# End of the eight FFNs in a two-block decoder kernel: a third buffer for the inner values, other order of the last down products, down weights of the last piece split in column halves

## The chip, the cores and the metric

One Trainium2 chip, one core. The time is the device time of one execution in microseconds (us). Three runs of the kernel before are known, with the median 2170.97 us. The profile is of one execution of its own, taken by the hardware profiler. Engines are named as in the profile: PE (TensorE, matrix products), PEld (its weight loads), DVE (VectorE), ACT (ScalarE), POOL (GpSimd), SP (SyncE, which here only issues DMAs).

## The reference

The input is 256 tokens of width 1024. Two model blocks, each of depth 2, run one behind the other. Every layer has two feed-forward networks (FFN) of inner width 2816 around a mixer, so there are eight FFNs. The part that the change touches is the FFN, and, in the second block's even mixer, the places of three small constant masks.

```python
def rmsnorm(x, g):
    xf = x.astype(jnp.float32)
    y = xf * lax.rsqrt(jnp.mean(xf * xf, axis=-1, keepdims=True) + EPS)
    return (y * g.astype(jnp.float32)).astype(x.dtype)

def swiglu_ffn(x, w_gu, w_down):
    gate, up = jnp.split(x @ w_gu, 2, axis=-1)
    return (jax.nn.silu(gate) * up) @ w_down

for i in range(DEPTH):
    x = x + 0.5 * swiglu_ffn(rmsnorm(x, ffn1_norm[i]), ffn1_w_gu[i], ffn1_w_down[i])
    xn = rmsnorm(x, mix_norm[i])
    x = x + mixer(xn, ...)
    x = x + 0.5 * swiglu_ffn(rmsnorm(x, ffn2_norm[i]), ffn2_w_gu[i], ffn2_w_down[i])
...
# second block, even mixer, gated delta rule in chunks of 64:
t_inv = lax.linalg.triangular_solve(a_low + eye, jnp.broadcast_to(eye, a_low.shape),
                                    left_side=True, lower=True, unit_diagonal=True)
```

## The kernel before

The stages run in the order f1.0, ab, f2.0, f1.1, nsa, f2.1, g1.0, ev, g2.0, pl0, g1.1, od, g2.1, pl1. Those named f or g are the FFNs: f2.0 and f2.1 have another FFN right behind them, the other six a mixer or a "ple" stage.

Every float32 product is made of three products of rounded parts: a value v is kept as its high part H (rounded by a copy to the type fp32r) and its low part L = v - H, and `mm3` adds H times H, H times L and L times H. So each weight costs ACT a copy (`hi`, into the tile WH) and DVE or POOL a subtraction (`lo`, into WL). Weights come in pieces through a ring of three slots, filled by SP in one fixed order. SP waits with a slot's next load until the low parts of its old contents are made.

**An FFN.** It has 22 pieces j. A piece holds 128 inner columns: 1024 weight columns for the gate product (part 0), 1024 for the up product (part 1), and 1024 for the down product (part 2). Per piece PE makes gate j, up j, and then the down products of piece j - 2, which wait for nothing by then. In between ACT and DVE form the inner value h = silu(gate) * up in `H`, its high part in `HH` and its low part in `HL` (the tiles HHt and HLt), each with two buffers that take turns by j % 2. A down product is `down(P, j, n, i)`: column half n (512 of the 1024 output columns) for the token half i (128 of 256 tokens), three matmuls with 512 columns each. The four accumulate in four banks of PSUM over all pieces (`acc00`, `acc10`, `acc01`, `acc11`).

**The end of an FFN** in the kernel before. In the last piece (21) PE makes the gate product, then the four down products of piece 19, then the up product. Behind it stand three of the four down products of piece 20 (nine matmuls), then `down_last(0)`, the six matmuls of piece 21 for the first column half, which wait for h's high part of each token half and only then for its low part; then the fourth down product of piece 20; then `follow[t].pe(P, 0)`, eight transposes of the first half of the new X ("flips" here) for the next stage; then `down_last(1)`. DVE adds the finished banks to X: `fin00` and `fin10` release the adds that the flips wait for. From the flips' results ACT and DVE make the next stage's input parts XH and XL (tile XBt), on which the next stage's first product waits.

ACT makes the high part of the last down weights (`hi(A, f"{t}.{j}", (2,))`) between the silu and the copy of the up product, as in every piece; DVE makes their low part right behind its gate work.

What sets the order of the work is the program order of each engine: no scheduler stands between. Semaphore waits are written by name.

**The masks.** In the even mixer POOL adds the left and the right half of three constant tables (`lev`, `bdT`, the identity) into `LEV`, `BD` and `ID` in the tile work before the solve. The constants come in two DMAs; the second, `ct1`, with 2173 columns, is issued by SP behind the loads of piece 3 and ahead of those of piece 4.

Of the kernel before, what the change touches and what calls it, by code (L numbers as in the profile page):

```python
# [6 lines left out]
F32 = mybir.dt.float32  # L7
# [17 lines left out]
def plan():  # L25
# [30 lines left out]
       ("cmneg", 30), ("mask4", 512), ("cos", 32), ("sin", 32), ("blk", 128), ("one1", 1)]  # L56

# [190 lines left out]
def build(nc, wts, vecs, rows4, rowb, cons, rgw, xin, out):  # L248
    ctx = ExitStack()
    with ctx:  # L250
# [3 lines left out]
        CO, NC = offsets(CON)  # L254
# [4 lines left out]
        HHt, HLt = sb("HHt", [128, 512], R32), sb("HLt", [128, 512], R32)  # L259
# [456 lines left out]
        def ffn(t, g, prev):  # L716
# [3 lines left out]
            HH, HL = v3(HHt[:, :], 2), v3(HLt[:, :], 2)  # L720
# [3 lines left out]
            def down(P, j, n, i):  # L724
                piece = f"{t}.{j}"
                wh, wl = wide(piece)
                P.wait_ge(f"{t}.hl{j}", f"{piece}:lo2", *ps.free(f"{t}.acc{i}{n}"), f"{t}.rbe")
                ws = slice(2048 + n * 512, 2560 + n * 512)
                P.mm3(ps[f"{t}.acc{i}{n}"], HH[:, j % 2, hs(i)], HL[:, j % 2, hs(i)], wh[:, ws], wl[:, ws], j == 0, False,
                      inc=f"{piece}:d" if n and i else None)  # L730

            def down_last(P, n):

                j, piece = NFF - 1, last
                wh, wl = wide(piece)
                ws = slice(2048 + n * 512, 2560 + n * 512)
                P.wait_ge(f"{piece}:lo2")
                for i in range(2):
                    P.wait_ge(f"{t}.hh{j}{i}")
                    P.mm(ps[f"{t}.acc{i}{n}"], HH[:, j % 2, hs(i)], wh[:, ws], False, False)  # L740
                    P.mm(ps[f"{t}.acc{i}{n}"], HH[:, j % 2, hs(i)], wl[:, ws], False, False)
                for i in range(2):
                    P.wait_ge(f"{t}.hl{j}{i}")
                    P.mm(ps[f"{t}.acc{i}{n}"], HL[:, j % 2, hs(i)], wh[:, ws], False, True,
                         inc=f"{piece}:d" if n and i else f"{t}.fin{i}{n}")
# [17 lines left out]
            def pe(P):  # L763
                if first:
                    norm.pe(P, 0)
                for j in range(NFF):
                    for u in range(2):
                        ps.take(f"{t}.{'gu'[u]}{j}")
                    for kts in (range(2), range(2, 4), range(4, 6), range(6, 8)) if j == 0 else (range(8),):
                        for u in range(2):  # L770
                            P.wait_ge(f"{t}.{j}:lo{u}", *ps.free(f"{t}.{'gu'[u]}{j}"))
                            if j == 1 and u == 1:
                                product(P, j, u, range(4))
                                row_pe(P, t, f"{t}.acc11")
                                product(P, j, u, range(4, 8))
                            else:
                                product(P, j, u, kts)
                            if j == NFF - 1 and u == 0:
                                for n in range(2):
                                    for i in range(2):  # L780
                                        down(P, j - 2, n, i)
                        if j == 0 and kts[0] == 0:
                            norm.pe(P, 1)
# [8 lines left out]
                for n, i in ((0, 0), (0, 1), (1, 0)):  # L792
                    down(P, NFF - 2, n, i)
                down_last(P, 0)
                down(P, NFF - 2, 1, 1)
                for i in range(2):
                    ps.give(f"{t}.acc{i}0", f"{t}.x{i}0")
                if t in follow:
                    follow[t].pe(P, 0)
# [4 lines left out]
            def act(A):  # L804
# [6 lines left out]
                for j in range(NFF):  # L811
# [7 lines left out]
                    hi(A, f"{t}.{j}", (2,))  # L819
# [5 lines left out]
                    if j < NFF - 1:  # L825
                        A.wait_ge(f"{t}.h{j}")
                        if j >= 2:
                            A.wait_ge(f"{t}.{j - 2}:d")
                        A.act(HH[:, b, :], H[:, b, :], ACT.Copy, inc=f"{t}.hh{j}")
                    else:  # L830
                        for i in range(2):
                            A.wait_ge(f"{t}.h{j}{i}", f"{t}.{j - 2}:d")
                            A.act(HH[:, b, hs(i)], H[:, b, hs(i)], ACT.Copy, inc=f"{t}.hh{j}{i}")
                        hi(A, nx2, (1,))
# [6 lines left out]
            def dve(V):  # L841
# [7 lines left out]
                for j in range(NFF):  # L849
# [13 lines left out]
                    lo(V, f"{t}.{j}", (2,))  # L863
# [25 lines left out]
                for i in range(2):  # L889
                    V.wait_ge(f"{t}.hh{j}{i}")  # L890
                    V.tt(HL[:, b, hs(i)], H[:, b, hs(i)], HH[:, b, hs(i)].bitcast(F32), SUB, inc=f"{t}.hl{j}{i}")
# [157 lines left out]
        def ab_mixer(prev):  # L1049
# [29 lines left out]
            YH, YL = v3(HHt[:, :], 2), v3(HLt[:, :], 2)  # L1079
# [889 lines left out]
        def even_mixer(prev):  # L1969
# [22 lines left out]
            LEV, BD, ID = v3(at(11776, 384), 6), at(12160, 64), at(12224, 64)  # L1992
# [554 lines left out]
            def dve(V):  # L2547
# [70 lines left out]
                for i in range(2):  # L2618
                    V.wait_ge(f"ev.xe{i}", "ev.blocks")
# [73 lines left out]
            def pool(G_):  # L2693
                G_.wait_ge(f"{t}.dg")
                G_.tt(LEV, v3(con("lev"), 6)[:, :, 0:64], v3(con("lev"), 6)[:, :, 64:128], ADD)
                G_.tt(BD, bdT[:, 0:64], bdT[:, 64:128], ADD, back=2)
                G_.tt(ID, IDN[:, 0:64], IDN[:, 64:128], ADD, inc="ev.blocks", back=3)
# [396 lines left out]
        def sync(S):  # L3094
# [8 lines left out]
            for name, n, two in PL:  # L3103
# [40 lines left out]
                if k == 3:  # L3144
                    S.dma(ct[:, 256:], cons[:, 256:], "cons1", inc="ct1")
# [213 lines left out]
```

## Time and profile before

| what | value |
|---|---|
| median of three runs | 2170.97 us (2170.86 to 2172.56) |
| span of the profiled execution, first to last instruction | 2171.1 us |
| PE busy | 2117.3 us, 98% of the span |
| DVE, ACT busy | 1548.0 us (71%), 1291.5 us (59%) |
| POOL busy | 73.2 us (3%) |
| moved by DMA | 363.00 MB, mean 167 GB/s |

The profiled execution has no time of its own beside its span; the span stands 0.1 us above the median of the runs. A busy share of 98% leaves PE about 54 us without an instruction in the whole program (2171.1 less 2117.3).

The rows below are in three forms. In a timeline a row begins with the start in us and the length of the row in us; behind them come engine, line and operation, out<-in by the tiles' names, and in brackets how long the engine sat idle before and what ended that. Matmuls overlap in such rows (one of 0.39 us may be followed by the next 0.23 us later), so it is starts that are compared, not lengths. In a table by form a row ends with busy us, mean ns of one, and idle time before. In a table of waits: us in total, times, longest.

### The profile page before, as it was taken

How to read it: one execution, taken by the hardware profiler on the slowest of the kernel's cores; microseconds unless marked ns; L12 is line 12 of the kernel's file. 1: busy time of each engine (PE TensorE's matmuls, PEld its weight loads, DVE VectorE, ACT ScalarE, POOL GpSimd, SP SyncE). 2: the span in 40 equal slices, each digit the busy share in tenths (PEclk: the TensorE clock that was granted, in tenths of full speed). 3: DMA queues.
4: the chain of work that ended last, by engine and by line, in shares of the span. 5: the costliest groups of instructions: out<-in, count | busy, mean ns of one | idle time of the engine just before them, and what ended most of it. 6: DMA issues, size and time to landing. Idle time of an engine off the chain costs nothing.

```text
span 2171.1 us, 33763 instructions
## 1 busy us (share of the span) xinstructions
PE 2117.3 (98%) x12655; PEld 1810.4 (83%) x12655; DVE 1548.0 (71%) x2771; ACT 1291.5 (59%) x2165; POOL 73.2 (3%) x49
## 2 busy tenths in 40 slices
PE   8999999999999989999999999999999999999998
PEld 7888988888888966888788897888887888988887
DVE  6777887677776576776777766577666776867676
ACT  6665766555555266655565666456555655666554
POOL 0001000000002300000000000000000000000001
PEclk9999999999999999999999998999999999999999
DMA  7453445554554532455455341145544554435552
GB/s 269 176 204 141 150 172 182 197 186 166 202 183 163 198 123 78 175 196 192 149 201 200 115 166 60 60 152 209 183 160 175 204 197 153 156 146 187 182 200 81
DMA packets 65532, 363.00 MB, mean 167 GB/s; under 512 B 7576, under 2 KB 8344, under 8 KB 33880
## 3 DMA queue, kind: packets, MB, share of 16 engines
q1 hardware_dynamic: 64944, 360.31, 46.1%
q8 instruction: 99, 1.62, 0.3%
q14 instruction: 65, 0.53, 0.1%
q0 software_dynamic: 128, 0.26, 0.0%
q10 hardware_dynamic: 296, 0.27, 0.0%
HBM read 359.77 MB, written 1.05 MB: 166 GB/s over the span
## 4 chain that ended last, share of the span: by engine, by line
PE 84%; DVE 10%; ACT 4%; issue 1%; DMA 0%; DVEq 0%; POOL 0%; ACTq 0%; SPq 0%; POOLq 0%
PE ps L202 83%; DVE WL L120 4%; PE ps L207 2%; DVE work L120 1%; ACT work L192 1%; ACT XBt L192 1%; DVE XBt L131 1%; ACT WH L192 1%; DVE small L131 1%; DVE work L131 1%; DVE small L120 1%; DVE work L157 0%; DVE work L125 0%; DVE small L127 0%; DVE XBt L120 0%
## 5 line engine op out<-in xcount | busy, mean ns | idle before, releaser
L202 PE MATMUL ps<-XBt,WH 128*128 128x512 f32 (+1 forms) x4208 | 1213.4, 355 | 13.2 <-DVE WL L120 6.6
L120 DVE TENSOR_TENSOR WL<-ring,WH 128x1024 fp32r<-128x1024 f32 (+1 forms) x642 | 789.3, 1229 | 364.3 <-ACT WH L192 320.3
L192 ACT ACTIVATE WH<-ring 128x1024 fp32r<-128x1024 f32 (+1 forms) x662 | 701.3, 1059 | 336.8 <-PE ps L202 269.5
L202 PE MATMUL ps<-XBt,WL 128*128 128x256 f32 x3384 | 896.0, 280 | 0.0
L202 PEld LDWEIGHTS ps<-XBt,WH 128*128 128x128 f32 x4208 | 729.4, 190 | 122.7 <-DVE XBt L131 9.8
L202 PEld LDWEIGHTS ps<-XBt,WL 128*128 128x128 f32 x3384 | 641.8, 190 | 26.2
L202 PE MATMUL ps<-WH,HHt 128*128 128x512 f32 x712 | 279.3, 392 | 1.3 <-DVE WL L120 0.7
L202 PE MATMUL ps<-WL,HHt 128*128 128x512 f32 x712 | 277.2, 389 | 0.0
L202 PE MATMUL ps<-WH,HLt 128*128 128x512 f32 x712 | 274.6, 389 | 0.0
L192 ACT ACTIVATE work<-ps 128x256 f32<-128x256 f32 (+5 forms) x457 | 184.3, 408 | 76.6 <-PE ps L202 39.6
L192 ACT ACTIVATE work<-work 128x256 f32<-128x256 f32 (+6 forms) x221 | 98.3, 445 | 183.3 <-DVE work L120 179.9
L120 DVE TENSOR_TENSOR work<-ps,work 128x256 f32<-128x256 f32 (+3 forms) x376 | 166.2, 442 | 42.9 <-PE ps L202 3.3
L202 PE MATMUL ps<-WH,XBt 128*128 128x512 f32 (+3 forms) x528 | 169.6, 391 | 12.9 <-DVE WL L120 11.1
L192 ACT ACTIVATE HHt<-work 128x256 fp32r<-128x256 f32 (+1 forms) x185 | 76.1, 411 | 147.0 <-DVE work L120 146.9
L202 PEld LDWEIGHTS ps<-WH,HLt 128*128 128x128 f32 x712 | 133.7, 188 | 28.9
L202 PEld LDWEIGHTS ps<-WL,HHt 128*128 128x128 f32 x712 | 133.8, 188 | 28.3
L202 PEld LDWEIGHTS ps<-WH,HHt 128*128 128x128 f32 x712 | 133.7, 188 | 24.2 <-DVE work L120 1.7
L120 DVE TENSOR_TENSOR work<-work 128x256 f32<-128x256 f32 (+2 forms) x338 | 142.8, 423 | 12.3 <-ACT work L192 0.7
L202 PEld LDWEIGHTS ps<-WH,XBt 128*128 128x128 f32 x528 | 99.9, 193 | 37.6 <-DVE WL L120 12.0
L120 POOL TENSOR_TENSOR WL<-ring,WH 128x1024 fp32r<-128x1024 f32 x22 | 53.8, 2448 | 1952.7 <-DVE HLt L120 1410.5
L202 PE MATMUL ps<-work 64*64 64x64 f32 (+16 forms) x1256 | 115.7, 278 | 3.9 <-ACT work L192 1.9
L202 PEld LDWEIGHTS ps<-work 64*64 64x64 f32 (+6 forms) x1256 | 87.5, 156 | 26.9 <-issue 10.9
(132 smaller groups left out, 1152.2 us busy)
## 6 DMA issues: line engine op xcount, KB each, us to landing
ring<-wts SPq DMA_DIRECT2D x244, 1024.0 KB, 5.9
ring<-wts SPq DMA_DIRECT2D x187, 512.0 KB, 3.8
ring<-wts SPq DMA_DIRECT2D x1, 1152.0 KB, 5.1
ct<-cons SPq DMA_DIRECT2D x1, 1086.5 KB, 5.8
Xt<-x SPq DMA_DIRECT2D x4, 256.0 KB, 5.3
out<-Xt SPq DMA_DIRECT2D x4, 256.0 KB, 2.0
work<-wts SPq DMA_DIRECT2D x1, 512.0 KB, 4.7
ring<-wts SPq DMA_DIRECT2D x1, 288.0 KB, 5.1
```

What stands on the lines that cost most here:

```text
L120: self.done(self.e and self.e.tensor_tensor(out, a, b, op), inc)
L131: self.done(self.e and self.e.scalar_tensor_tensor(out, a, s, b, op0, op1), inc)
L192: self.done(self.e and self.e.activation(out, a, f, **kw), inc)
L202: inst = self.e and self.e.matmul(out, l, r, start=start, stop=stop)
L207: inst = self.e and self.e.transpose(out, a, ident)
```

## The change

HHt and HLt grow from two buffers to three; the third is used by the last piece alone. The four down products of piece 19 are moved behind the last up product too, where those of piece 20 stood already, and two of piece 20's now stand between `down_last(0)` and the flips. The order behind the up product is four of piece 19, two of piece 20 (column half 0), `down_last(0)`, two of piece 20 (column half 1), flips, `down_last(1)`. `down_last` now waits for h's low part and uses `mm3`. The last down weights are split into high and low part in two halves of 512 columns, on both engines behind the work on h. The masks' half tables are loaded by DMA into the places where they are used, in seven more DMAs from the same source; POOL's three additions and the wait for them are gone.

```diff
+HALF = {"lev": 384}
+CHIP = [(n, HALF.get(n, c)) for n, c in CON] + [("bd2", 64), ("id2", 64)]
...
-        HHt, HLt = sb("HHt", [128, 512], R32), sb("HLt", [128, 512], R32)
+        HHt, HLt = sb("HHt", [128, 768], R32), sb("HLt", [128, 768], R32)
...
             def down_last(P, n):
...
-                P.wait_ge(f"{piece}:lo2")
-                for i in range(2):
-                    P.wait_ge(f"{t}.hh{j}{i}")
-                    P.mm(ps[f"{t}.acc{i}{n}"], HH[:, j % 2, hs(i)], wh[:, ws], False, False)
-                    P.mm(ps[f"{t}.acc{i}{n}"], HH[:, j % 2, hs(i)], wl[:, ws], False, False)
+                P.wait_ge(f"{piece}:lo2{'' if n else 'a'}")
                 for i in range(2):
                     P.wait_ge(f"{t}.hl{j}{i}")
-                    P.mm(ps[f"{t}.acc{i}{n}"], HL[:, j % 2, hs(i)], wh[:, ws], False, True,
-                         inc=f"{piece}:d" if n and i else f"{t}.fin{i}{n}")
+                    P.mm3(ps[f"{t}.acc{i}{n}"], HH[:, 2, hs(i)], HL[:, 2, hs(i)], wh[:, ws], wl[:, ws], False, True,
+                          inc=f"{piece}:d" if n and i else f"{t}.fin{i}{n}")
+
+            def split_last_act(A, n):
+
+                wh, _, w = cut(last, 2)
+                s = slice(n * 512, n * 512 + 512)
+                A.wait_ge(loaded(last, 2), f"{t}.{NFF - 3}:d{'' if n else '0'}")
+                A.act(wh[:, s], w[:, s], ACT.Copy, inc=f"{last}:hi2{'' if n else 'a'}")
+
+            def split_last_dve(V, n):
+                wh, wl, w = cut(last, 2)
+                s = slice(n * 512, n * 512 + 512)
+                V.wait_ge(f"{last}:hi2{'' if n else 'a'}")
+                V.tt(wl[:, s], w[:, s], wh[:, s].bitcast(F32), SUB, inc=f"{last}:lo2{'' if n else 'a'}")
...
-                            if j == NFF - 1 and u == 0:
-                                for n in range(2):
-                                    for i in range(2):
-                                        down(P, j - 2, n, i)
...
-                for n, i in ((0, 0), (0, 1), (1, 0)):
-                    down(P, NFF - 2, n, i)
+                for n in range(2):
+                    for i in range(2):
+                        down(P, NFF - 3, n, i)
+                for i in range(2):
+                    down(P, NFF - 2, 0, i)
                 down_last(P, 0)
-                down(P, NFF - 2, 1, 1)
                 for i in range(2):
                     ps.give(f"{t}.acc{i}0", f"{t}.x{i}0")
+                for i in range(2):
+                    down(P, NFF - 2, 1, i)
                 if t in follow:
                     follow[t].pe(P, 0)
                 down_last(P, 1)
...
-                            A.wait_ge(f"{t}.h{j}{i}", f"{t}.{j - 2}:d")
-                            A.act(HH[:, b, hs(i)], H[:, b, hs(i)], ACT.Copy, inc=f"{t}.hh{j}{i}")
+                            A.wait_ge(f"{t}.h{j}{i}")
+                            A.act(HH[:, 2, hs(i)], H[:, b, hs(i)], ACT.Copy, inc=f"{t}.hh{j}{i}")
+                        for n in range(2):
+                            split_last_act(A, n)
                         hi(A, nx2, (1,))
...
+                for n in range(2):
+                    split_last_dve(V, n)
...
-                G_.wait_ge(f"{t}.dg")
-                G_.tt(LEV, v3(con("lev"), 6)[:, :, 0:64], v3(con("lev"), 6)[:, :, 64:128], ADD)
-                G_.tt(BD, bdT[:, 0:64], bdT[:, 64:128], ADD, back=2)
-                G_.tt(ID, IDN[:, 0:64], IDN[:, 64:128], ADD, inc="ev.blocks", back=3)
...
-                    S.dma(ct[:, 256:], cons[:, 256:], "cons1", inc="ct1")
+                    a, b = offsets(CON)[0], offsets(CON)[1]
+                    lev, tail = a["lev"][0], a["cm01"][0]
+                    S.dma(ct[:, 256:lev], cons[:, 256:lev], "cons1")
+                    for e in range(2):
+                        r = slice(64 * e, 64 * e + 64)
+                        S.dma(v3(con("lev")[r, :], 6), v3(cons[r, lev:tail], 6)[:, :, 64 * e:64 * e + 64], "cons1")
+                        S.dma(con("bd2")[r, :], cons[r, a["bdT"][0] + 64 * e:a["bdT"][0] + 64 * e + 64], "cons1")
+                        S.dma(con("id2")[r, :], cons[r, 64 * e:64 * e + 64], "cons1")
+                    S.dma(ct[:, tail - 384:CO["bd2"][0]], cons[:, tail:b], "cons1", inc="ct1")
```

PE at the end of the first FFN (f1.0), before. Here ps6 and ps7 are the banks acc00 and acc10 (column half 0), ps0 and ps1 are acc01 and acc11. The rows begin with the third down product of piece 20, behind the last up product:

```order
L202 MATMUL ps0<-WH,HHt 128x512
L202 MATMUL ps0<-WL,HHt 128x512
L202 MATMUL ps0<-WH,HLt 128x512
L202 MATMUL ps6<-WH,HHt 128x512 [waits scalar_done,vector_done]
L202 MATMUL ps6<-WL,HHt 128x512
L202 MATMUL ps7<-WH,HHt 128x512 [waits scalar_done]
L202 MATMUL ps7<-WL,HHt 128x512
L202 MATMUL ps6<-WH,HLt 128x512 [waits vector_done]
L202 MATMUL ps7<-WH,HLt 128x512 [waits vector_done]
L202 MATMUL ps1<-WH,HHt 128x512
L202 MATMUL ps1<-WL,HHt 128x512
L202 MATMUL ps1<-WH,HLt 128x512
```

PE at the same place, after, from the second down product of piece 20 to the third. Ahead of these rows stand the up product and fifteen more matmuls of down products:

```order
L204 MATMUL ps7<-WH,HHt 128x512
L204 MATMUL ps7<-WL,HHt 128x512
L204 MATMUL ps7<-WH,HLt 128x512
L204 MATMUL ps6<-WH,HHt 128x512 [waits vector_done]
L204 MATMUL ps6<-WL,HHt 128x512
L204 MATMUL ps6<-WH,HLt 128x512
L204 MATMUL ps7<-WH,HHt 128x512
L204 MATMUL ps7<-WL,HHt 128x512
L204 MATMUL ps7<-WH,HLt 128x512
L204 MATMUL ps0<-WH,HHt 128x512
L204 MATMUL ps0<-WL,HHt 128x512
L204 MATMUL ps0<-WH,HLt 128x512
```

The last piece's first half has one wait now in place of four, on DVE's low parts; it stands behind 18 matmuls of down products instead of nine, counted from the end of the up product, and six matmuls instead of three follow it before the flips.

ACT at the same place, before, from the silu of piece 21 (work<-work) on:

```order
L192 ACTIVATE work<-work 128x256 [waits scalar_done,vector_done]
L192 ACTIVATE WH<-ring 128x1024 [waits scalar_done,matmul_done,rear0]
L192 ACTIVATE work<-ps5 128x256 [waits scalar_done,matmul_done]
L192 ACTIVATE HHt<-work 128x128 [waits scalar_done,vector_done] x2
L192 ACTIVATE WH<-ring 128x1024 [waits scalar_done]
```

and after:

```order
L194 ACTIVATE work<-work 128x256 [waits scalar_done,vector_done]
L194 ACTIVATE work<-ps5 128x256 [waits scalar_done,matmul_done]
L194 ACTIVATE HHt<-work 128x128 [waits scalar_done,vector_done] x2
L194 ACTIVATE WH<-ring 128x512 [waits scalar_done,matmul_done,rear0]
L194 ACTIVATE WH<-ring 128x512 [waits scalar_done,matmul_done]
L194 ACTIVATE WH<-ring 128x1024 [waits scalar_done]
```

The high part of the last down weights has moved from ahead of the copy of the up product (work<-ps5) to behind the high part of h, in two halves. DVE's low part has moved in the same way.

SP in the first FFN, after; before, the six rows on ct are one, `L195 DMA ct<-cons 128x2173`:

```order
L197 DMA ring<-wts 128x2048 [waits vector_done]
L197 DMA ring<-wts 128x1024 [waits vector_done]
L197 DMA ct<-cons 128x640
L197 DMA ct<-cons 64x6x64
L197 DMA ct<-cons 64x64 x2
L197 DMA ct<-cons 64x6x64
L197 DMA ct<-cons 64x64 x2
L197 DMA ct<-cons 128x765
L197 DMA ring<-wts 128x2048
```

The load of piece 4's gate and up weights (the last row) stands behind eight DMAs of constants instead of one.

## Rows read from the trace of the kernel before

**Rows 1.** The page: its head, and the chain that ended last, by engine

```profile
span 2171.1 us, 33763 instructions
...
PE 84%; DVE 10%; ACT 4%; issue 1%; DMA 0%; DVEq 0%; POOL 0%; ACTq 0%; SPq 0%; POOLq 0%
```

**Rows 2.** Waits of PE over the whole span, longest in total

```profile
PE ps L202 <- DVE WL L120: 18.4, 14, 3.8
```

**Rows 3.** Timeline, end of f2.0 (an FFN follows): PE and ACT

```profile
497.65 0.42 ACT L192 ACTIVATE work<-work 128x256 f32<-128x256 f32 x1 [0.80 <-DVE work L120]
...
499.57 0.40 PE L202 MATMUL ps<-WH,HHt 128*128 128x512 f32 x1
...
502.26 0.47 PE L202 MATMUL ps<-WH,HHt 128*128 128x512 f32 x1 [0.47 <-ACT HHt L192]
...
504.63 1.31 PE L207 MATMUL ps<-ct,Xt 128*128 128x128 f32 x8
505.70 0.48 PE L202 MATMUL ps<-WH,HHt 128*128 128x512 f32 x1
...
507.56 0.50 PE L202 MATMUL ps<-XBt,WH 128*128 128x256 f32 x2 [0.23 <-DVE XBt L131]
```

**Rows 4.** Timeline, end of f1.1 (a mixer follows): ACT, DVE and PE

```profile
685.05 0.42 ACT L192 ACTIVATE work<-work 128x256 f32<-128x256 f32 x1
...
687.69 0.40 PE L202 MATMUL ps<-WH,HHt 128*128 128x512 f32 x1
687.89 0.39 ACT L192 ACTIVATE work<-ps 128x256 f32<-128x256 f32 x1 [1.25 <-PE ps L202]
...
689.68 0.69 DVE L120 TENSOR_TENSOR HLt<-work,HHt 128x128 fp32r<-128x128 f32 x2
689.75 0.39 PE L202 MATMUL ps<-WH,HHt 128*128 128x512 f32 x1
...
691.89 1.31 PE L207 MATMUL ps<-ct,Xt 128*128 128x128 f32 x8
692.96 0.48 PE L202 MATMUL ps<-WH,HHt 128*128 128x512 f32 x1
...
696.36 1.04 PE L207 MATMUL ps<-ct,Xt 128*128 128x128 f32 x8
...
697.32 0.50 PE L202 MATMUL ps<-XBt,WH 128*128 128x256 f32 x2
```

**Rows 5.** Timeline, ends of f2.1 (two rows) and g1.0 (three rows)

```profile
1044.99 0.40 PE L202 MATMUL ps<-WH,HHt 128*128 128x512 f32 x1
...
1050.77 0.48 PE L202 MATMUL ps<-WH,HHt 128*128 128x512 f32 x1
...
1234.31 0.42 ACT L192 ACTIVATE work<-work 128x256 f32<-128x256 f32 x1 [0.64 <-DVE work L120]
...
1236.40 0.40 PE L202 MATMUL ps<-WH,HHt 128*128 128x512 f32 x1
...
1242.02 0.48 PE L202 MATMUL ps<-WH,HHt 128*128 128x512 f32 x1
```

**Rows 6.** Groups by form, whole span: work of 512 columns on ACT and DVE

```profile
L192 ACT ACTIVATE work<-Xt 128x512 f32<-128x512 f32 x60 | 38.0, 633 | 6.1 <-DVE Xt L120 0.5 <-DVE XBt L131 0.4
...
L120 DVE TENSOR_TENSOR work<-ps,work 128x512 f32<-128x512 f32 x24 | 16.6, 692 | 4.7 <-PE ps L202 2.3 <-DVE small L139 0.5
```

**Rows 7.** Timeline, first FFN: SP's DMA issues, then ACT, DVE, PE

```profile
30.05 0.44 SPq L195 DMA_DIRECT2D ct<-cons  x1
30.53 0.43 SPq L195 DMA_DIRECT2D ring<-wts  x1
...
38.39 1.06 ACT L192 ACTIVATE WH<-ring 128x1024 fp32r<-128x1024 f32 x1 [2.29 <-DMA ring<-wts]
...
43.48 1.23 DVE L120 TENSOR_TENSOR WL<-ring,WH 128x1024 fp32r<-128x1024 f32 x1
...
46.77 0.63 PE L202 MATMUL ps<-XBt,WH 128*128 128x512 f32 x2
```

More of the change, by code:

```diff
@@ L253, in build @@
         RO, NR = offsets(ROW)
-        CO, NC = offsets(CON)
+        CO, NC = offsets(CHIP)
         ring = sb("ring", [128, NSLOT * SLOT])
@@ L719, in ffn @@
             SG, H, GU, LW = v3(buf(512), 2), v3(buf(512), 2), v3(buf(1024), 2), v3(buf(1024), 2)
-            HH, HL = v3(HHt[:, :], 2), v3(HLt[:, :], 2)
+            HH, HL = v3(HHt[:, :], 3), v3(HLt[:, :], 3)
             first = t == "f1.0"
@@ L729, in down @@
                 P.mm3(ps[f"{t}.acc{i}{n}"], HH[:, j % 2, hs(i)], HL[:, j % 2, hs(i)], wh[:, ws], wl[:, ws], j == 0, False,
-                      inc=f"{piece}:d" if n and i else None)
+                      inc=f"{piece}:d" if n and i else f"{piece}:d0" if i and j == NFF - 3 else None)
             def down_last(P, n):
@@ L818, in act @@
                     A.act(SG[:, b, :], GU[:, b, 0:256], ACT.Silu, inc=f"{t}.sg{j}")
-                    hi(A, f"{t}.{j}", (2,))
+                    if j < NFF - 1:
+                        hi(A, f"{t}.{j}", (2,))
                     if j >= NARROW:
@@ L862, in dve @@
                         lo(V, nx2, (0,) if j else (1,))
-                    lo(V, f"{t}.{j}", (2,))
+                    if j < NFF - 1:
+                        lo(V, f"{t}.{j}", (2,))
                     V.wait_ge(f"{t}.sg{j}")
@@ L890, in dve @@
                     V.wait_ge(f"{t}.hh{j}{i}")
[L891 removed]
+                    V.tt(HL[:, 2, hs(i)], H[:, b, hs(i)], HH[:, 2, hs(i)].bitcast(F32), SUB, inc=f"{t}.hl{j}{i}")
+                for n in range(2):
+                    split_last_dve(V, n)
                 for n in range(2):
@@ L1078, in ab_mixer @@
             wif, wil = HHt[:, 0:64], HLt[:, 0:64]
-            YH, YL = v3(HHt[:, :], 2), v3(HLt[:, :], 2)
+            YH, YL = v3(HHt[:, 0:512], 2), v3(HLt[:, 0:512], 2)
             def if_pe(P):
@@ L1991, in even_mixer @@
                                          for a in (11264, 12288, 13312, 14336, 15360, 16384)]
-            LEV, BD, ID = v3(at(11776, 384), 6), at(12160, 64), at(12224, 64)
+            LEV, BD, ID = v3(con("lev"), 6), con("bd2"), con("id2")
             WT, S_ = two_(2048), at(3072, 512)
@@ L2618, in dve @@
                 for i in range(2):
-                    V.wait_ge(f"ev.xe{i}", "ev.blocks")
+                    V.wait_ge(f"ev.xe{i}")
                     for h in range(4):
```

## Prediction

> **What bounds the kernel now.** I read the page's head and its chain first, then PE's waits, then the timelines of all eight FFN ends, then the start, where SP's order changes. The span is 2171.1 us and 84% of the chain that ended last is PE itself [rows 1]. So time goes only where PE's matmul count goes (this change leaves it as it is) or where PE stands still. PE's longest sum of waits is for low parts of weights made by DVE, 18.4 us in 14 places [rows 2]. At the FFN ends, where this change works, PE waits far less, and that is the point on which everything hangs.
>
> I call U the start of the first down product behind the last up product, and D the start of `down_last(1)`, behind the flips. From U to D PE has 18 matmuls of 512 columns and eight transposes. At the end of f1.1, U is 687.69, `down_last(0)` starts at 689.75 after nine matmuls (2.06 us, 0.229 us each, so without a wait), and D is 692.96 [rows 4]: U to D is 5.27 us. Four other ends (f1.0, g2.0, g1.1, g2.1) have the same shape with 5.27 or 5.28 us. At the end of f2.0 `down_last(0)` starts at 502.26, 2.69 us behind U at 499.57, after the same nine matmuls: a stall of 0.63 us for h's high part, and more inside `down_last(0)`, since D is 505.70, U plus 6.13 us [rows 3]. For f2.1 U to D is 5.78 us, for g1.0 it is 5.62 us [rows 5]. So five of the eight ends have next to nothing to gain, and the other three hold 0.96, 0.61 and 0.45 us above a floor that I work out now.
>
> **The floor.** 18 matmuls at 0.229 us are 4.12 us. Nine plus nine before bring the f1.1 flips to 687.69 + 4.12 = 691.81; they start at 691.89, so 0.08 us goes on the change of work. The flips then take 1.07 us to D there, because their second token half waits for X; the next stage's flips, which wait for nothing, take 0.96 us (696.36 to 697.32), and their own rows say the same, 1.04 against 1.31 us [rows 4]. After the change X's two adds are ready before the flips, since six matmuls (1.37 us) stand between `down_last(0)` and them. The floor is 4.12 + 0.08 + 0.96 = 5.16 us.
>
> **When can the new `down_last(0)` start?** PE reaches it after the four down products of piece 19 and two of piece 20. U's meaning shifts with the change: the up product now comes 12 matmuls earlier, and the instant at which piece 19's products end and those of piece 20 begin is where U was. So PE reaches `down_last(0)` at U + 6 x 0.229 = U + 1.37 us. It needs h's low part and the low part of the first 512 columns of the down weights.
>
> The up product ends 2.7 us earlier, yet ACT cannot take it at once: it sits in the silu of piece 21, which waits for DVE and which the change doesn't touch. From the silu's end on: ACT copies the up product, then comes the work on h. Before, from the start of that copy to the end of h's low parts, it is 687.89 to 689.68 + 0.69 = 690.37, so 2.48 us [rows 4]. ACT's new half copy begins about 0.45 us before that end (at the end of h's second high part) and takes 0.63 us; DVE's half subtraction follows 0.04 us later and takes 0.69 us [rows 6]. That is the copy's start plus 2.48 - 0.45 + 0.63 + 0.04 + 0.69, about 3.4 us.
> - f1.1: silu from 685.05, 0.42 long, copy at 685.51, low part at 688.93. PE arrives at 687.69 + 1.37 = 689.06. No stall, with some 0.08 us to spare after 0.05 us of signalling. The same at the four ends of its shape.
> - f2.0: silu from 497.65, copy at 498.11, low part at 501.53, PE arrives at 500.94. A stall of 0.59, plus 0.13 us for the signal and the slower first matmul behind a wait: 0.72 us. f2.1 has the shape of f2.0, and I give it the same 0.72 us.
> - g1.0: silu from 1234.31, copy at 1234.77, low part at 1238.19, PE arrives at 1237.77: 0.42 + 0.13 = 0.55 us.
>
> So the change cuts the chain by less than it seems: it brings the up product forward by 2.7 us, but it moves the down weights' split behind h, and makes PE wait for all low parts where before it could start on the high ones.
>
> **The sum at the FFN ends**, each against U to D before: five ends 5.16 against 5.27, 0.11 us gained each, 0.55 in all. f2.0: 5.16 + 0.72 = 5.88 against 6.13, 0.25 gained. f2.1: 5.88 against 5.78, 0.10 lost. g1.0: 5.71 against 5.62, 0.09 lost. Net gain 0.61 us. Behind D the next product waits for the flips' way over ACT and DVE, 1.86 us from D at f2.0 (505.70 to 507.56), and not for `down_last(1)` [rows 3]. That way is unchanged and starts with the flips, so a shift of D passes on whole and no more is to be had. The bounds of this term: with no stall anywhere it gains 0.55 + 0.97 + 0.62 + 0.46 = 2.6 us; if DVE could begin only when ACT has made both halves (0.67 us later), it loses about 5 x 0.59 + 3 x 0.67 - 0.6 = 4.4 us. I take 0.61, since both half durations have rows of their own size.
>
> What else moves at the ends: the last piece's low down part frees its ring slot about 1.8 us later, so where an FFN follows, SP issues two loads later. They serve pieces 2 and 3 of the next FFN, wanted more than 10 us behind; cost nothing. POOL's splits for the next mixer start earlier, which nobody waits for. The third buffers take away a wait of ACT for piece 19's products, which in the new order would have come late; by themselves they gain nothing.
>
> **The start.** SP issues the constants at 30.05 in 0.44 us and piece 4's load at 30.53 [rows 7]. Seven more DMAs at 0.43 us put that load about 3.0 us later. Before, it queued behind more than a megabyte of constants and landed when ACT's wait ended, at 38.39 [rows 7]; so issued 3 us later it finds the queue nearly empty, and I expect it to land between 0 and 3 us later. What lies over it: DVE's last low part made from that load runs 43.48 to 44.71, and the up product that needs it starts at 47.00, the second matmul of the row at 46.77 [rows 7]. That is 2.3 us of cover. No row of before shows such a strided load by SP. At three us of delay the cost is 0.7 us (3.0 - 2.3); if each of the seven takes twice the issue time of the row, the load is 6.0 us late and costs 3.7 us. I take 0, by the queue that is empty by then. The bytes shrink a little, so below zero there is nothing but tenths, and those are covered as well.
> The Trainium skill speaks against these small DMAs ("DMA: Bandwidth & Descriptors", section Bandwidth): it advises large transfers and calls those under 64 KB "descriptor-dominated"; its table has 64 KB at 0.95 us. Four of the new ones are 16 KB and two 98 KB. By an estimate from that page, some 0.9 us for each of six, one behind the other, the load would land up to 5.4 us later and the sum would be 2173.5 instead. No row here shows it either way.
>
> **The masks.** POOL's three additions and DVE's wait for them go. POOL is in 0% of the chain [rows 1], they are done long before they are read, and the removed wait had been met. Cost and gain 0.
>
> **Sum:** 2171.1 - 0.61 = 2170.5 for the profiled span. That span stands 0.1 above the median of 2170.97, so in terms of the median 2170.4 us.
>
> **Rivals.**
> 1. *The low parts come late (slower).* Place: the first matmul of `down_last(0)`, all eight ends. If the chain of h and the half splits is x us longer than I reckon, three ends lose x and five lose x - 0.08. The gain of 0.61 is gone at x = 0.13. For it: the slack at five ends is a twelfth of a microsecond, and ACT and DVE must take turns four times within it. Against: every link has a measured duration. With x = 0.35 the time is 2170.4 + 8 x 0.35 - 0.4 = 2172.8; at its bound, 0.67, it is 2175.4.
> 2. *The constants' DMAs hold up piece 4 (slower).* It decides from 2.3 us of delay on, and outweighs the gain from 2.9 us. For it: ACT already waited 2.29 us for this load before the change [rows 7], so it is the tightest load of the program. With the 6.0 us from above PE loses 3.7 us: 2170.4 + 3.7 = 2174.1. Against: the bytes are fewer, and the load is alone in the queue once it is issued.
> 3. *All stalls go (faster).* If silu 21 ended earlier too, or DVE took the half split sooner, every end would sit on the floor: 2171.0 - 2.6 = 2168.4. For it: the up product is 2.7 us earlier. Against: silu 21 hangs on the gate work, which stands where it stood.
> 4. *Nothing reaches the end.* If the ACT and DVE way behind the flips also waits for something else, the tenths vanish: 2171.0. It can't be told from the forecast.
>
> **Chances.** Forecast with rival 4: 0.74 (own range 2169.4 to 2171.8). Rival 1: 0.11. Rival 2: 0.07. Rival 3: 0.08. A measurement can tell from no change about 0.2%, 4.3 us, so faster means under 2166.6 and slower over 2175.3. No worked case reaches the first, only the far end of rival 1 or rivals 1 and 2 together reach the second. For what I have overlooked I leave 0.04 faster, 0.05 slower, 0.91 within. The range, 2168.2 to 2173.4, takes in rival 3, the middle of rival 1 and rival 2 up to 5.3 us of delay.
>
> **What would show it.** In the profile after: U to D of 5.2 us at the five ends, with no wait ahead of `down_last(0)`; 5.9 at f2.0 and f2.1 and 5.7 at g1.0, with a wait for DVE's WL of about 0.6 us there; D to the next product still 1.86 us; piece 4's high part in the first FFN at 38 to 41 us, and PE without a gap near 47. Wrong would be: waits for DVE WL at all eight ends (rival 1), a gap at 44 to 50 us (rival 2), or ends of 5.2 us everywhere (rival 3).

## The result, and the profile after

| | kernel before | changed kernel |
|---|---|---|
| median of the runs | 2170.91 us (2169.51 to 2172.56, 4 runs) | 2188.63 us (2183.20 to 2189.84, 4 runs) |
| span of the profiled execution | 2171.1 us | 2186.2 us (its time as a run: 2187.99) |

The changed kernel takes 1.0072 times as long, with the interval 1.0061 to 1.0084: 13 to 18 us slower. The medians are 17.7 us apart, the spans of the two profiled executions 15.1 us. The forecast was 2170.4 us, with a range of 2168.2 to 2173.4.

The head of the page after, with its line of the chain (engine, busy us, share, instructions):

```profile
span 2186.2 us, 33797 instructions
...
PE 2116.9 (97%) x12655; PEld 1810.6 (83%) x12655; DVE 1565.9 (72%) x2779; ACT 1291.9 (59%) x2173; POOL 72.4 (3%) x46
...
PE 79%; DVE 12%; ACT 6%; issue 2%; DMA 0%; SPq 0%; DVEq 0%; ACTq 0%; POOL 0%; POOLq 0%
```

Against [rows 1] PE has the same work (2116.9 against 2117.3 us), so nearly all of the 15.1 us is time in which it stands still. DVE has become 17.9 us busier (1565.9 against 1548.0), though the change gives it no more to subtract. The table of waits and the table by form say where. First PE's waits for DVE's low parts after the change (us, times, longest), against 18.4 us in 14 before [rows 2]:

```profile
PE ps L204 <- DVE WL L122: 30.9, 23, 3.8
```

Then, of the table by form, the half splits that the change made (busy us, mean ns; idle before):

```profile
L122 DVE TENSOR_TENSOR WL<-ring,WH 128x512 fp32r<-128x512 f32 x16 | 29.2, 1825 | 3.5 <-ACT WH L194 2.6
```

An operation of this size had a row with 692 ns before [rows 6]; here the sixteen have a mean of 1825 ns. They cost 29.2 where 16 x 0.692 = 11.1 us were due: 18.1 us too much, which accounts for the 17.9 us that DVE gained. The timeline of the end of f1.1 shows a case (start, length, what):

```profile
691.89 0.69 DVE L122 TENSOR_TENSOR HLt<-work,HHt 128x128 fp32r<-128x128 f32 x2
...
692.17 0.39 PE L204 MATMUL ps<-WH,HHt 128*128 128x512 f32 x1
...
692.72 5.16 POOL L122 TENSOR_TENSOR WL<-ring,WH 128x1024 fp32r<-128x1024 f32 x2 [473.00 <-DVE HLt L122]
...
692.91 5.52 DVE L122 TENSOR_TENSOR WL<-ring,WH 128x512 fp32r<-128x512 f32 x2 [0.33 <-ACT WH L194]
...
695.69 0.50 PE L204 MATMUL ps<-WH,HHt 128*128 128x512 f32 x1 [2.00 <-DVE WL L122]
...
698.55 1.41 DVE L133 SCALAR_TENSOR_TENSOR Xt<-ps,small,Xt 128x512 f32<-128x512 f32 x2
...
699.35 1.32 PE L209 MATMUL ps<-ct,Xt 128*128 128x128 f32 x8 [0.65 <-DVE Xt L133]
...
700.42 0.48 PE L204 MATMUL ps<-WH,HHt 128*128 128x512 f32 x1
```

POOL waits for h's low part (the semaphore `{t}.hl{NFF - 1}1`) before it makes two splits for the next mixer. DVE has to wait a little longer, for ACT's high part. So POOL starts at 692.72 and DVE at 692.91, 0.19 us behind; DVE's first half then takes 2.73 us and ends at 695.63, 0.55 us behind POOL's first split, and PE stands still for 2.00 us ahead of `down_last(0)`. POOL's second split is then in progress, so DVE's second half takes as long again; behind it come the adds into X, and the flips wait 0.65 us more. From U (692.17) to D (700.42) it is 8.25 us, where 5.27 stood before [rows 4].

Where no such POOL split is ready, the forecast holds. The same place at f2.0, whose next stage is another FFN:

```profile
504.39 0.39 PE L204 MATMUL ps<-WH,HHt 128*128 128x512 f32 x1
...
505.83 1.49 DVE L122 TENSOR_TENSOR WL<-ring,WH 128x512 fp32r<-128x512 f32 x2 [0.33 <-ACT WH L194]
...
506.58 0.50 PE L204 MATMUL ps<-WH,HHt 128*128 128x512 f32 x1 [0.66 <-DVE WL L122]
...
509.46 1.04 PE L209 MATMUL ps<-ct,Xt 128*128 128x128 f32 x8
510.25 0.48 PE L204 MATMUL ps<-WH,HHt 128*128 128x512 f32 x1
```

Both halves in 1.49 us, a wait of 0.66 us, and U to D is 5.86 us; the forecast was 5.88, with [rows 3] at 6.13. The five ends at which POOL starts a split right behind h's low part (f1.0, f1.1, g2.0, g1.1, g2.1) have the long wait of f1.1, with one difference: at g1.1 POOL makes a single split, so that only DVE's first half is held up (both halves together take 3.46 us there, against 5.52 at f1.1). The other three are like f2.0. At g1.0 POOL has a split too, but it waits for ACT and starts at 1245.64, behind DVE's halves (1243.63 to 1245.12). U to D of each in us, starts of matmuls compared as in the prediction (6.12 and 5.77 are from unrounded starts; the rows give 6.13 and 5.78):

| | f1.0 | f2.0 | f1.1 | f2.1 | g1.0 | g2.0 | g1.1 | g2.1 |
|---|---|---|---|---|---|---|---|---|
| before | 5.27 | 6.12 | 5.27 | 5.77 | 5.62 | 5.27 | 5.27 | 5.27 |
| forecast | 5.16 | 5.88 | 5.16 | 5.88 | 5.71 | 5.16 | 5.16 | 5.16 |
| changed | 8.88 | 5.86 | 8.25 | 5.86 | 5.66 | 8.20 | 8.68 | 8.20 |

From U to the next stage's first product, the eight ends together grow from 59.07 to 75.14 us, by 16.1. Two of the five bad ends, f1.0 and g1.1, lose half a microsecond more than the others, g1.1 although only one half was held up. There the clock fell. The table of windows gives the granted clock behind the engines' busy times:

```profile
200.20:203.40 3.20, 3.20 (x10) 2.42 (x9) 2.75 (x3) 0.00 (x0) 0.80 (x1) 0.50 0.62 256
...
1855.70:1858.90 3.20, 3.20 (x9) 2.46 (x8) 1.50 (x2) 0.00 (x0) 0.00 (x0) 0.50 0.72 289
```

0.50 is 1.2 GHz, half of 2.4. In these 3.2 us, which begin about 1 us after PE's wait ended (1.4 us at f1.0, 0.8 at g1.1), matmuls of 512 columns start 0.43 us apart instead of 0.23. At g1.1 it is 5.23 us from `down_last(0)` to D, where the same stretch takes 3.65 us at the full clock in `pool_behind` below, so about 1.6 us of that end is the clock. At f1.0 it is about 0.5 us (5.25 us from `down_last(0)` to D against 4.73 at f1.1), since the flips wait for X there anyway.

The start is the second place. SP's constants and the loads behind them, and ACT's high part of the first piece 4 load, against [rows 7]:

```profile
30.02 5.10 SPq L197 DMA_DIRECT2D ct<-cons  x8
...
35.16 24.93 SPq L197 DMA_DIRECT2D ring<-wts  x9
...
41.82 1.06 ACT L194 ACTIVATE WH<-ring 128x1024 fp32r<-128x1024 f32 x1 [5.75 <-DMA ring<-wts]
...
48.19 0.50 PE L204 MATMUL ps<-XBt,WH 128*128 128x512 f32 x1 [0.91 <-DVE WL L122]
```

Eight DMAs took SP 5.10 us, 0.64 each and not 0.43; the high part began at 41.82 instead of 38.39, and PE stood still for 0.91 us. U of f1.0 is 1.3 us later than before (195.19 against 193.88). So the ledger of the span is +16.1 at the ends, +1.3 at the start, and 15.1 - 16.1 - 1.3 = -2.3 us in the mixers between. The change doesn't touch that part, and the profiles differ there by as much anyway: `masks_alone` (below) has the same ends as before and a start 0.4 us later, and yet a span of 2168.1 us, 3 less. Of the 2.3 us, 1.7 lie in the nsa mixer (344.3 us between the same two matmuls, against 346.0), where the profile before has 6.8 us at half clock and the changed kernel's has none; that of `masks_alone` has none there either, and takes 344.6 us.

### The profile page after: what moved, and what is told of

Its sections match the earlier page's. It is cut to its first block, busy times and chain, and to the rows that moved or that the text cites. A ratio compares the mean times of both kernels' runs of the same rounds, so it can differ in the third digit from the quotient of the medians.

```text
span 2186.2 us, 33797 instructions
## 1 busy us (share of the span) xinstructions
PE 2116.9 (97%) x12655; PEld 1810.6 (83%) x12655; DVE 1565.9 (72%) x2779; ACT 1291.9 (59%) x2173; POOL 72.4 (3%) x46
## 4 chain that ended last, share of the span: by engine, by line
PE 79%; DVE 12%; ACT 6%; issue 2%; DMA 0%; SPq 0%; DVEq 0%; ACTq 0%; POOL 0%; POOLq 0%
PE ps L204 77%; DVE WL L122 6%; ACT WH L194 2%; DVE work L122 2%; ACT work L194 2%; PE ps L209 2%; ACT XBt L194 1%; DVE XBt L133 1%; DVE small L133 1%; DVE work L133 1%; DVE small L122 1%; DVE work L159 0%; DMA ring<-wts 0%; SPq L197 0%; DVE work L127 0%
## 5 line engine op out<-in xcount | busy, mean ns | idle before, releaser
L122 DVE TENSOR_TENSOR WL<-ring,WH 128x1024 fp32r<-128x1024 f32 (+1 forms) x650 | 807.6, 1243 | 356.3 <-ACT WH L194 312.0
L194 ACT ACTIVATE WH<-ring 128x1024 fp32r<-128x1024 f32 (+2 forms) x670 | 702.9, 1049 | 341.5 <-PE ps L204 268.5
L204 PE MATMUL ps<-WH,XBt 128*128 128x512 f32 (+3 forms) x528 | 168.5, 388 | 13.1 <-DVE WL L122 11.1
```

What stands on the lines that cost most here:

```text
L122: self.done(self.e and self.e.tensor_tensor(out, a, b, op), inc)
L194: self.done(self.e and self.e.activation(out, a, f, **kw), inc)
L204: inst = self.e and self.e.matmul(out, l, r, start=start, stop=stop)
```

## The experiments

The theory: DVE's subtraction with two operands in SBUF and POOL's split exclude each other, and the one that starts first holds the other up to its end. Before the change DVE's last such operation at these five ends, ahead of the adds, was h's low part, and just for this POOL waited. The change puts two more behind it and leaves POOL's wait as it was. The rivals: the half split is slow for a reason of its own (its size, ACT writing the other half of the tile beside it); or the order on PE, the waits in `mm3` or the constants cost the time.

The first four kernels ran together on one chip, the last two on another; each ratio is against runs of the kernel before on the same chip.

**`pool_behind`: the changed kernel, POOL starts behind both halves.**

```diff
-                G.wait_ge(f"{t}.hl{NFF - 1}1")
+                G.wait_ge(f"{last}:lo2")
```

> The changed kernel, but POOL begins its two splits for the next mixer only when DVE has made both halves of the last low part, not when h's low part is made. Theory (DVE and POOL exclude each other while both read two SBUF operands; POOL's 2.5 us splits now start just ahead of DVE's half splits): the half splits return from 2.7 to 0.7 us each at the five ends with a mixer behind, PE's wait ahead of the last piece goes there, and the time falls from 2188.6 to 2170.5 to 2173 us, with about 1.2 us left over from the start. Rival 1 (the chain h, half copy, half split is simply too long in the new order): the five ends keep their 2 us waits, 2187 us or more. Rival 2 (the half form into WL is slow by itself): half splits stay at 1.8 us in the mean, 2187 us.

Measured: 2171.12 us (11 runs) against 2172.21, ratio 0.9997 (0.9988 to 1.0005). Its table by form and its waits:

```profile
L122 DVE TENSOR_TENSOR WL<-ring,WH 128x512 fp32r<-128x512 f32 x16 | 11.1, 692 | 3.5 <-ACT WH L194 2.7
```

```profile
PE ps L204 <- DVE WL L122: 20.1, 17, 3.8
```

The same sixteen halves beside the same work of ACT take 692 ns each. One line, and the whole loss is gone, as expected (2170.5 to 2173 us), with the order on PE, `mm3` and the constants as changed. The end of f1.1, on DVE, POOL and PE in turn:

```profile
687.90 1.49 DVE L122 TENSOR_TENSOR WL<-ring,WH 128x512 fp32r<-128x512 f32 x2 [0.33 <-ACT WH L194]
689.65 1.44 DVE L133 SCALAR_TENSOR_TENSOR Xt<-ps,small,Xt 128x512 f32<-128x512 f32 x2 [0.26 <-PE ps L204]
...
689.53 4.92 POOL L122 TENSOR_TENSOR WL<-ring,WH 128x1024 fp32r<-128x1024 f32 x2 [474.83 <-DVE WL L122]
...
688.65 0.50 PE L204 MATMUL ps<-WH,HHt 128*128 128x512 f32 x1
688.98 0.40 PE L204 MATMUL ps<-WL,HHt 128*128 128x512 f32 x1
...
691.50 1.03 PE L209 MATMUL ps<-ct,Xt 128*128 128x128 f32 x8
692.29 0.48 PE L204 MATMUL ps<-WH,HHt 128*128 128x512 f32 x1
```

DVE's adds into X run beside POOL (689.65 to 691.09, POOL from 689.53) and take 1.44 us, about as long as behind it (1.41 at f1.1 in the changed kernel): they have one operand in PSUM. So it is the operations with two operands in SBUF that are held up, not DVE as such. U to D at the five ends is 5.17, 5.13, 5.15, 5.13 and 5.17 us; f2.0, f2.1 and g1.0 are 5.88, 5.86 and 5.69.

**`pool_between`: POOL starts behind the first half.** As above, but with `f"{last}:lo2a"`.

> The changed kernel, but POOL begins behind DVE's first half split and ahead of its second. Theory: the first half split takes 0.7 us and the last piece's products start without a wait, but the second half split stands behind POOL's first one (about 2.5 us longer), and with it DVE's two adds into X, which are behind it in DVE's order; the flips wait for them. About 1 us lost at each of the five ends: 2176 to 2180 us. Rival (only what the last piece waits for matters): as with POOL behind both, 2171 to 2173 us.

Measured: 2175.26 us (10 runs), ratio 1.0014 (1.0005 to 1.0023), a little below the 2176 to 2180 expected, since only three of the five ends lost anything. The sixteen halves have a mean of 1112 ns. At g2.0, g1.1 and g2.1 U to D is 6.46, 6.44 and 6.45 us; at f1.0 and f1.1 it is 5.16 and 5.13, with nothing lost. The two cases, f1.1 and g2.1:

```profile
688.66 1.49 DVE L122 TENSOR_TENSOR WL<-ring,WH 128x512 fp32r<-128x512 f32 x2 [0.33 <-ACT WH L194]
...
689.49 5.45 POOL L122 TENSOR_TENSOR WL<-ring,WH 128x1024 fp32r<-128x1024 f32 x2 [474.04 <-ACT WH L194]
...
2137.02 3.73 DVE L122 TENSOR_TENSOR WL<-ring,WH 128x512 fp32r<-128x512 f32 x2 [0.33 <-ACT WH L194]
...
2137.80 5.18 POOL L122 TENSOR_TENSOR WL<-ring,WH 128x1024 fp32r<-128x1024 f32 x2 [290.29 <-DVE WL L122]
...
2140.87 1.41 DVE L133 SCALAR_TENSOR_TENSOR Xt<-ps,small,Xt 128x512 f32<-128x512 f32 x2
...
2141.68 1.31 PE L209 MATMUL ps<-ct,Xt 128*128 128x128 f32 x8 [0.87 <-DVE Xt L133]
```

At g2.1 POOL came first: DVE's two halves take 3.73 instead of 1.49 us. At f1.1 POOL also waited for ACT's high part, so DVE's second half was first by some 0.04 us, and now POOL is the one that is longer, 5.45 instead of 4.92 us. Who starts first wins, either way round. The two engines are ready within 0.02 to 0.25 us of each other in these runs, so such an order isn't fixed by the program: it is a race for time, which any change elsewhere may tip.

**`pool_early`: the kernel before, POOL starts earlier.** This puts the collision into the old code and leaves all else alone.

```diff
-                G.wait_ge(f"{t}.hl{NFF - 1}1")
+                G.wait_ge(f"{t}.h{NFF - 2}")
```

> The kernel before, unchanged but for one wait: POOL begins its first split for the next mixer when h of piece 20 is made, 6 us earlier, while DVE still has work with two SBUF operands to do (the low part of h20, the gate's scaling, the last down weights' low part). Theory: the first such DVE operation stands still until POOL's split ends, about 2 us, and the whole chain of piece 21 is that much later; the slack at these ends is some 0.5 us, so 1 to 2 us lost at each of the ends with a mixer behind: 2175 to 2180 us. Rival (exclusion is no property of the two engines, only of the new order): 2170.9 us, and no DVE operation is longer than before.

Measured: 2178.23 us (5 runs), ratio 1.0032 (1.0019 to 1.0044), as expected. At the end of f1.1, the low part of h in piece 20:

```profile
684.33 2.40 POOL L120 TENSOR_TENSOR WL<-ring,WH 128x1024 fp32r<-128x1024 f32 x1 [468.14 <-DVE work L120]
...
684.67 2.34 DVE L120 TENSOR_TENSOR HLt<-work,HHt 128x256 fp32r<-128x256 f32 x1 [0.48 <-ACT HHt L192]
...
687.11 0.42 DVE L120 TENSOR_TENSOR work<-ps,work 128x256 f32<-128x256 f32 x1
```

In the kernel before, the same operation:

```profile
683.36 0.43 DVE L120 TENSOR_TENSOR HLt<-work,HHt 128x256 fp32r<-128x256 f32 x1 [0.48 <-ACT HHt L192]
```

0.43 us become 2.34, and it ends 0.28 us behind POOL (687.01 against 686.73). So the cause is neither the size of 512 columns nor the changed kernel's order. U to D grows by 1.4 to 1.6 us at the same five ends (6.87, 6.74, 6.67, 6.67, 6.67) and stays at the other three.

**`masks_alone`: the kernel before with the masks by DMA.** The eight DMAs, the half tables and the removed additions, as in the diff of the change; the FFNs as before.

> The kernel before with the masks' part of the change alone: eight DMAs of constants ahead of piece 4's load, no additions on POOL. Theory: the eight issues take 5.1 us of SP instead of 0.4, piece 4 lands 3.4 us later, PE stands still for about 1 us near 47 us, and nothing else changes: 2171.8 to 2172.5 us. Rival (the start costs nothing in the end, because the backlog is caught up): 2170.9 us. Rival (the masks change the even mixer too): a shift of more than 0.5 us between 1240 and 1460 us.

Measured: 2172.91 us (11 runs), ratio 1.0004 (0.9995 to 1.0013): it can't be told from nothing, and 1.3 us can't be either. The gap of PE near 47 us that was expected isn't in its profile, has SP's constants in the same time and ACT's wait for the load shorter than in the changed kernel (5.75):

```profile
30.30 5.09 SPq L197 DMA_DIRECT2D ct<-cons  x8
```

```profile
40.90 1.06 ACT L194 ACTIVATE WH<-ring 128x1024 fp32r<-128x1024 f32 x1 [4.54 <-DMA ring<-wts]
```

With 4.5 us of wait, here and in `pool_behind` and `pool_between`, PE has no gap; with 5.75 it has 0.91 us. From issue to landing this load took 6.64 us in the changed kernel's profile and 5.39 to 5.46 in the other three; why stays open. The second rival's shift of more than 0.5 us in the even mixer is there, but it isn't the masks': between the same two matmuls, near 1244 and 1460 us, it is 215.9 us before and 214.2 in this profile, but 215.9 in `pool_behind`, which has the same masks, and 214.3 in `pool_early`, which has the old ones. The two short ones have less time at half clock there, 17.0 and 20.4 us against 23.8 in the other two. The FFN part alone wasn't tried: the third buffers take the room that the masks' half tables give back.

**`behind_later`: `pool_behind` with the constants' DMAs two pieces later** (`if k == 5` for `if k == 3` in SP's order).

> The kernel with POOL behind both half splits, and the eight DMAs of constants issued two pieces later, behind the loads of piece 5. Theory: the remaining cost of the change is the delay of piece 4's load at the start (1.2 us of PE in the changed kernel's profile, about 0.4 us in that of the masks alone); with it gone the time is 0.5 to 1.2 us below that of the kernel with POOL behind and 0.5 to 1 us below the kernel before: about 0.9995 of it. Rival (the load that now stands behind the constants is as tight): no change against POOL behind.

Measured: 2172.26 us (11 runs) against 2172.68, ratio 1.0001 (0.9992 to 1.0010). No gain that can be measured; the half of a tenth of a per cent that was expected is smaller than the interval, so it is neither shown nor excluded. ACT's long wait for a load has moved to the piece behind the constants and is shorter (2.84 us).

**`low_last`: `behind_later`, with `down_last` using what is ready first.** The high part's products of both token halves come first, and DVE's low part of the weights is wanted four matmuls later.

```diff
+                for i in range(2):
+                    P.wait_ge(f"{t}.hl{j}{i}", f"{piece}:hi2{'' if n else 'a'}")
+                    P.mm(ps[f"{t}.acc{i}{n}"], HH[:, 2, hs(i)], wh[:, ws], False, False)
+                    P.mm(ps[f"{t}.acc{i}{n}"], HL[:, 2, hs(i)], wh[:, ws], False, False)
+                P.wait_ge(f"{piece}:lo2{'' if n else 'a'}")
                 for i in range(2):
-                    P.wait_ge(f"{t}.hl{j}{i}")
-                    P.mm3(ps[f"{t}.acc{i}{n}"], HH[:, 2, hs(i)], HL[:, 2, hs(i)], wh[:, ws], wl[:, ws], False, True,
-                          inc=f"{piece}:d" if n and i else f"{t}.fin{i}{n}")
+                    P.mm(ps[f"{t}.acc{i}{n}"], HH[:, 2, hs(i)], wl[:, ws], False, True,
+                         inc=f"{piece}:d" if n and i else f"{t}.fin{i}{n}")
```

> The same kernel, and within each column half of the last piece the two products with the low part of the weights come last instead of second, so that PE can begin with the high parts before DVE's half split is ready. Theory: the stalls of 0.6 to 0.7 us ahead of the last piece at f2.0, f2.1 and g1.0 go, since four matmuls (0.9 us) cover them; 2.0 us less than the kernel with only POOL and constants moved, 0.9985 to 0.999 of the kernel before. Rival (the flips are held up by DVE's adds into X anyway, as DVE's second half split stands ahead of them): no change, because the adds start no earlier.

Measured: 2167.01 us (2164.87 to 2169.38, 11 runs), ratio 0.9975 (0.9967 to 0.9984): 5 us faster than the kernel before, and some 21 faster than the change as it was made. That is more than the 2 us expected. PE at the end of f1.1:

```profile
687.53 0.39 PE L204 MATMUL ps<-WH,HLt 128*128 128x512 f32 x1
687.75 0.39 PE L204 MATMUL ps<-WH,HHt 128*128 128x512 f32 x1
687.98 0.39 PE L204 MATMUL ps<-WH,HLt 128*128 128x512 f32 x1
688.21 0.61 PE L204 MATMUL ps<-WL,HHt 128*128 128x512 f32 x2
688.66 0.39 PE L204 MATMUL ps<-WH,HHt 128*128 128x512 f32 x1
...
690.03 1.03 PE L209 MATMUL ps<-ct,Xt 128*128 128x128 f32 x8
690.82 0.48 PE L204 MATMUL ps<-WH,HHt 128*128 128x512 f32 x1
```

One matmul each 0.23 us and no gap into the flips. U to D is 4.87 to 4.88 us at the five ends, 5.20 at f2.0 and f2.1, 4.99 at g1.0; up to the next stage's first product the eight ends sum to 55.29 us, against 58.62 in `behind_later` and 59.07 before. That is 3.3 of the 5.3 us between these two kernels: 2.0 at the three ends that the expectation counted, and 0.25 at each of the five that it didn't. The other 2 us lie in the mixers, above all in the even one (213.0 us from near 1244 to near 1460, against 215.9), where this profile has 13.6 us at half clock against 23.8. The median granted clock of the eleven runs is 0.994 against 0.993, so this may hold for most of them; whether the shorter ends bring it about is open.

## Why the prediction was wrong, step by step

**The step that failed** is a clause: "POOL's splits for the next mixer start earlier, which nobody waits for". It was costed at nothing because no engine waits for their result. The engine that waits is DVE, for the way to SBUF that they occupy. The same mistake sits in the half split's price, "both half durations have rows of their own size". The size is right, but the row of 692 ns in [rows 6] is of another kind: work<-ps,work has one operand in PSUM, and the half split has both in SBUF. Three of that row's operations did run beside a POOL split and kept their time, such as this one in the kernel before:

```profile
735.80 2.40 POOL L120 TENSOR_TENSOR WL<-ring,WH 128x1024 fp32r<-128x1024 f32 x1 [11.54 <-ACT WH L192]
...
735.94 0.69 DVE L120 TENSOR_TENSOR work<-ps,work 128x512 f32<-128x512 f32 x1
```

So this row could never have shown what the half split would meet. With the half clock behind it (about 2.1 us of it, at f1.0 and g1.1), the clause cost 15.9 us of the 16.1 at the ends (the sum over the five of U to D after, less before), and it made the sign wrong. That the bound of the term was also too narrow (4.4 us of loss at most) follows from this: with POOL first, DVE's first half takes 2.66 to 2.84 us instead of 0.69 at all five ends, and at four of them the second half takes 2.68 to 2.71 us again.

The trace of before had the answer in rows that the prediction didn't use. At the end of g1.0, and behind the end of f1.1, POOL and DVE:

```profile
1240.40 2.38 POOL L120 TENSOR_TENSOR WL<-ring,WH 128x1024 fp32r<-128x1024 f32 x1 [482.60 <-ACT WH L192]
...
1241.66 1.21 DVE L120 TENSOR_TENSOR WL<-ring,WH 128x64 fp32r<-128x64 f32 x1
...
705.36 2.41 POOL L120 TENSOR_TENSOR WL<-ring,WH 128x1024 fp32r<-128x1024 f32 x1 [2.79 <-DVE work L125]
...
705.64 3.21 DVE L120 TENSOR_TENSOR WL<-ring,WH 128x1024 fp32r<-128x1024 f32 x1
```

A split of 64 columns takes 1.21 us, longer than one of 512, and ends at 1242.87, where POOL's ends at 1242.78. One of 1024 columns takes 3.21 us, where [rows 7] have 1.23, and ends at 708.85, 1.08 us behind POOL's (707.77). Held operations of 256, 512 and 1024 columns end 0.28, 0.55 and 1.08 us behind POOL's split in all these traces, each 0.14 us less than their own 0.42, 0.69 and 1.22 us: they do nearly all of their work after POOL's end. The Trainium skill states the rule ("SBUF — State Buffer", section "SBUF: two separate sides"): DVE and GpSimd share a pair of ports, it is an exclusive lock and not a split of bandwidth, and a DVE operation takes part in it when it has two inputs in SBUF and the GpSimd operation reads SBUF too; whichever starts first has it to its end. Every run here agrees: a half split goes from 0.69 to between 2.66 and 2.94 us behind POOL, h's low part from 0.43 to between 2.27 and 2.47 us, POOL's two splits go from 4.92 to 5.45 us behind DVE, and the adds with an operand in PSUM stay at 1.41 to 1.44 us.

**The order at the ends was right** where POOL was out of the way: 5.86, 5.86 and 5.66 us in the changed kernel against 5.88, 5.88 and 5.71, and 5.13 to 5.17 in `pool_behind` against 5.16 at the five. But 5.16 came out of two errors that cancel. I took 0.96 us for the flips and found no stall at the five ends; [rows 4] have 0.96 from the first flip to the next product, yet in `pool_behind` a flips' row of the same length (1.03) goes from 691.50 to 692.29, 0.79 us, so 0.17 us of the 0.96 weren't the flips'. And `down_last(0)` starts 1.49 us behind U instead of 1.37, with a slower first matmul (0.33 us to the next). Rival 1's mechanism was thus there at all eight ends, by a tenth of a microsecond at five. `low_last` took it away at these five, to 18 x 0.228 + 0.79 = 4.9 us, and this was worth more than the whole change in the form predicted. Of the 0.61 us forecast, `pool_behind` has 0.35 at the ends (58.72 us from U to the next stage's first product, against 59.07), too little to be seen in its time.

**From D to the next product** it stayed 1.86 or 1.87 us at six ends and 1.96 at f1.0. At g1.0 it grew from 2.03 to 2.39 us: ACT's next high part waits for piece 20's last down product, which the change put later. I had called this way unchanged.

**The start** was forecast at 0 (ends 0 and 3.7) and cost 1.3 us in the changed kernel's profile. In the others with the constants at the same place U of f1.0 is 0 to 0.75 us later than before and PE has no gap near 47 us; of the 0.75 in `pool_between` and the 0.4 in `masks_alone`, 0.6 and 0.25 were there before the first constant was issued. SP took 0.64 us for each DMA, not 0.43, so the load was issued 4.6 us later, not 3.0; that it landed only 3.4 us later fits the emptier queue that was argued (6.6 us from issue to landing against 7.8 before). Rival 2 was a third true. Against the estimate of 0.9 us for each small transfer, one behind the other, worked out from the Trainium skill's table ("DMA: Bandwidth & Descriptors", section Bandwidth; it is of DMAs issued from GpSimd, these are issued by SP), the delay was that of issuing: the six small transfers of the changed kernel landed 2.1 to 4.3 us after their issue and 0.2 to 0.3 us one behind the other.

**The masks** on POOL and DVE: nothing, as forecast. From near 1244 to near 1460 us the two are alike, 215.9 us in `pool_behind` and before.

**The rivals**: 3 fell, and 4 too at seven ends, where the way from D was unchanged. The case that came, slower by 13 to 18 us, was in none of them; the 0.05 that I left for slower had no mechanism behind it.

## What to carry to other kernels

A step that "nobody waits for" still occupies something. When a change moves work of DVE or POOL at all, list what the other of the two does in that window and look for operations of DVE with both operands in SBUF; in the trace before, look for one that is too long for its size. Then give the order between the two a semaphore of its own, as `pool_behind` does, so that it isn't left to a tenth of a microsecond. And put the product that needs the last-made operand last: that one reorder gave 5 us, and the whole restructuring without it nothing that can be measured. (The reorder alone, in the kernel before, wasn't tried.)

## What the runs showed of the hardware

- A DVE subtraction with two SBUF operands waits for a POOL split in progress to its end, and POOL for DVE likewise. DVE's of 64, 256, 512 and 1024 columns then take up to 1.22, 2.47, 2.94 and 3.21 us, and end 0.08, 0.28, 0.55 and 1.08 us behind POOL's split. Operations with one of their operands in PSUM keep their time beside POOL (0.69 us for 512 columns at 735.94 in the kernel before).
- PE's granted clock fell to 1.2 GHz for at least 3.2 us, about 1 us behind the end of a wait of 2 us, at two of five ends (f1.0, g1.1) and not at the other three, whose waits were of the same length. What sets these two apart the runs don't show.
- SP's eight DMAs of constants stand 0.64 us apart on average. The first, over 128 partitions, takes 0.43 us to issue, like the one large DMA before; the six over 64 partitions take 0.60 to 0.73, and the last, over 128 partitions again, 0.59. So the number of partitions alone doesn't decide it.
